# Where the operands of the large products begin in SBUF: a float32 block of delta-net, mixer and merge on one core

## The reference

```python
hdn = rms_norm(x, norm_g) * (1 + scale) + shift           # scale, shift, gate from silu(c) @ ada_w
qkv, z, b, a = split(hdn @ w_in)                          # 1024 x 6176: the delta-net's inputs
...                                                       # conv, silu, l2norm, chunked delta rule, 16 heads
x = x + gate * ((rms_norm(o) * silu(z)) @ w_out)          # 2048 -> 1024
x = rms_norm(x, final_g)
h = rms_norm(x, norm_pre)
proj = h @ w_in_2                                         # differential attention (4 heads) and mLSTM (4 heads)
...
merged = sigmoid(ga) * (ya @ w_a) + sigmoid(gb) * (yb @ w_b)
out = x + rms_norm(merged @ w_out_2, norm_post)
```

## Time and profile before

| | us |
|---|---|
| median of 3 runs | 2098.05 (2096.22 to 2102.33) |
| profiled execution | 2098.08 |
| its span, first to last instruction | 2096.3 |
| PE busy | 1992.0 |
| VectorE busy | 1273.6 |
| ScalarE busy | 853.6 |
| mean granted clock of TensorE | 0.985 |

### The profile page before, as it was taken

The page is one execution under the profiler, slowest core; times in us unless marked ns, Lnnn a source line. Parts: engine busy times, 40 slices in busy tenths (PEclk is TensorE's granted clock), DMA queues, the critical chain, the costliest instruction groups (busy, mean ns, idle before and its releaser), DMA issues.

```text
span 2096.3 us, 29439 instructions
## 1 busy us (share of the span) xinstructions
PE 1992.0 (95%) x11256; PEld 1618.5 (77%) x11256; DVE 1273.6 (61%) x2417; ACT 853.6 (41%) x1377; POOL 138.0 (7%) x114
## 2 busy tenths in 40 slices
PE   5989999999999999969999999999999999999998
PEld 2667878888887888857776787777777678888877
DVE  6777878796869686749625644445353435633543
ACT  4644353544344443149403333535343337600321
POOL 0020202011111212000000000000000000000000
PEclk8999999999999999989999999999999999999999
DMA  7222323232323242548313221120312125211232
GB/s 279 90 76 70 98 78 106 66 101 72 104 68 102 70 121 67 170 148 284 91 43 138 67 66 36 46 95 21 111 41 81 61 79 213 91 50 42 87 114 81
DMA packets 128971, 200.27 MB, mean 96 GB/s; under 512 B 56596, under 2 KB 88084, under 8 KB 127808
## 3 DMA queue, kind: packets, MB, share of 16 engines
q1 hardware_dynamic: 128832, 198.39, 29.6%
HBM read 156.22 MB, written 42.11 MB: 95 GB/s over the span
## 4 chain that ended last, share of the span: by engine, by line
PE 47%; DVE 4%; DMA 2%; issue 2%; ACT 1%; SPq 0%; DVEq 0%; ACTq 0%
PE m_job L1710 6%; PE m_job L1712 6%; PE m_job L1711 6%; PE e_b L2397 4%; PE e_b L2398 4%; PE e_b L2399 4%; PE p_out L1359 2%; PE p_sc L1956 2%; PE p_out L1361 2%; PE p_out L1360 2%; PE p_s L1979 2%; PE e_b L2468 1%; PE e_b L2467 1%; PE e_b L2466 1%; DMA m_raw<-in_w 1%
## 5 line engine op out<-in xcount | busy, mean ns | idle before, releaser
L795 PE MATMUL p_job<-h_hi,w_hi 128*128 128x512 f32 x768 | 321.7, 419 | 18.2 <-DVE h_lo L185 16.8
L797 PE MATMUL p_job<-h_hi,w_lo 128*128 128x512 f32 x768 | 302.6, 394 | 0.0
L796 PE MATMUL p_job<-h_lo,w_hi 128*128 128x512 f32 x768 | 302.1, 393 | 0.0
L1710 PE MATMUL m_job<-h_hi,m_hi 128*128 128x512 f32 x576 | 237.7, 413 | 2.8 <-issue 2.1
L1712 PE MATMUL m_job<-h_hi,m_lo 128*128 128x512 f32 x576 | 227.1, 394 | 0.0
L1711 PE MATMUL m_job<-h_lo,m_hi 128*128 128x512 f32 x576 | 226.0, 392 | 0.0
L795 PEld LDWEIGHTS p_job<-h_hi,w_hi 128*128 128x128 f32 x768 | 146.0, 190 | 59.3 <-issue 16.4
L796 PEld LDWEIGHTS p_job<-h_lo,w_hi 128*128 128x128 f32 x768 | 145.9, 190 | 35.1 <-issue 7.9
L797 PEld LDWEIGHTS p_job<-h_hi,w_lo 128*128 128x128 f32 x768 | 145.6, 190 | 31.3
L1710 PEld LDWEIGHTS m_job<-h_hi,m_hi 128*128 128x128 f32 x576 | 108.8, 189 | 49.8 <-issue 28.3
L633 ACT ACTIVATE pre<-p_job 128x512 f32<-128x512 f32 x96 | 56.7, 591 | 177.6 <-PE p_job L797 174.9
(11 more groups left out here) (398 smaller groups left out, 4170.1 us busy)
## 6 DMA issues: line engine op xcount, KB each, us to landing
w_raw<-in_w SPq DMA_DIRECT2D x49, 512.0 KB, 3.6
m_raw<-in_w SPq DMA_DIRECT2D x49, 512.0 KB, 3.7
rows<-grows SPq DMA_DIRECT2D x32, 512.0 KB, 6.8
ada<-in_ada_w SPq DMA_DIRECT2D x8, 1024.0 KB, 5.3
z_scr<-pre SPq DMA_DIRECT2D x16, 512.0 KB, 2.6
o_scr<-oT SPq DMA_DIRECT2D x64, 128.0 KB, 1.8
ob<-o_scr SPq DMA_DIRECT2D x16, 512.0 KB, 4.9
zb<-z_scr SPq DMA_DIRECT2D x16, 512.0 KB, 4.9
```

Source lines behind the costliest of these rows:

```text
L795: nc.tensor.matmul(bank, hi, h_hi[:, k, cut], start=(k == 0), stop=False)
L796: nc.tensor.matmul(bank, hi, h_lo[:, k, cut], start=False, stop=False)
L797: last = nc.tensor.matmul(bank, lo, h_hi[:, k, cut], start=False, stop=(k == KD - 1))
L1710: nc.tensor.matmul(bank, hi, h_hi[:, k, cut], start=(k == 0), stop=False)
```

## The change

The three small columns `eps`, `gate` and `rin_col` move behind `h_hi`, `h_lo` and the weight tiles, and are declared 64 bytes wide (`LINE` = 16 elements), as is `adt`; their users take slices of the former width. `w_raw`, `w_hi`, `w_lo` are declared for the whole program, and `m_raw`, `m_hi`, `m_lo` become names for the same tiles (they had the same addresses before). The scratch for descriptors shrinks from 16384 to 1024 bytes a partition.

```diff
@@ stage_norm
-            nc.vector.memset(keep["eps"][:], EPS).then_inc(eps_set, 1)
+            nc.vector.memset(keep["eps"][:, 0:1], EPS).then_inc(eps_set, 1)
@@ stage_deltanet
-                                nc.vector.tensor_tensor(keep["gate"][:], gsum[:], gbias[:], ALU.add)
+                                nc.vector.tensor_tensor(keep["gate"][:, 0:KD], gsum[:], gbias[:], ALU.add)
@@ stage_after
-    with ExitStack() as front:
-        for name, shape, dt in (("m_raw", [P, KD * P], F32), ("m_hi", [P, 2, KD * P], F32R),
-                                ("m_lo", [P, 2, KD * P], F32R)):
-            keep[name] = front.enter_context(nc.sbuf_tensor(name, shape, dt))
+    keep["m_raw"], keep["m_hi"], keep["m_lo"] = keep["w_raw"], keep["w_hi"], keep["w_lo"]
@@ build
-            "ident": sb("ident", [P, P]), "ones": sb("ones", [P, P]), "eps": sb("eps", [P, 1]),
-            "gate": sb("gate", [P, KD]), "rin_col": sb("rin_col", [P, NT]),
+            "ident": sb("ident", [P, P]), "ones": sb("ones", [P, P]),
             "h_hi": sb("h_hi", [P, KD, T], F32R), "h_lo": sb("h_lo", [P, KD, T], F32R),
+            "w_raw": sb("w_raw", [P, KD * P]), "w_hi": sb("w_hi", [P, 2, KD * P], F32R),
+            "w_lo": sb("w_lo", [P, 2, KD * P], F32R),
+            "eps": sb("eps", [P, LINE]), "gate": sb("gate", [P, LINE]), "rin_col": sb("rin_col", [P, LINE]),
...
-            for name, shape, dt in (("w_raw", [P, KD * P], F32), ("w_hi", [P, 2, KD * P], F32R),
-                                    ("w_lo", [P, 2, KD * P], F32R), ("tri", [P, P], F32),
-                                    ("conv_w", [P, QK_HEADS, 4, TAPS], F32), ("adt", [P, 3], F32)):
+            for name, shape, dt in (("tri", [P, P], F32), ("conv_w", [P, QK_HEADS, 4, TAPS], F32),
+                                    ("adt", [P, LINE], F32)):
@@ kernel
-    nc = bacc.Bacc("TRN2", target_bir_lowering=False, num_devices=1)
+    nc = bacc.Bacc("TRN2", target_bir_lowering=False, num_devices=1, dynamic_dma_scratch_size=1024)
```

More of the change, by code:

```diff
@@ L35 @@
 EPS = 1e-6
+LINE = 16
 QK_HEADS = 8
@@ L2608, in stage_after @@
     first, second, third = ExitStack(), ExitStack(), ExitStack()
-    with ExitStack() as front:
-        for name, shape, dt in (("m_raw", [P, KD * P], F32), ("m_hi", [P, 2, KD * P], F32R),
-                                ("m_lo", [P, 2, KD * P], F32R)):
-            keep[name] = front.enter_context(nc.sbuf_tensor(name, shape, dt))
[L2613 to L2618, removed]
+    keep["m_raw"], keep["m_hi"], keep["m_lo"] = keep["w_raw"], keep["w_hi"], keep["w_lo"]
+    with first:
+        out = stage_out(nc, io, keep, first)
+    with second:
+        mix = stage_mix(nc, io, keep, second)
+    with third:
+        merge = stage_merge(nc, io, keep, third, mix)
+    if True:
         with nc.Block() as block:
```

## The result

| | before | changed |
|---|---|---|
| median, us | 2097.62 (12 runs, 2095.0 to 2102.33) | 2100.93 (12 runs, 2096.93 to 2107.6) |
| ratio | | 1.0019, 95% interval 1.0011 to 1.0027 |
| profiled execution, us | 2098.08 | 2096.93 |

What follows compares the result with a forecast made beforehand. TensorE's list of 6528 fp32r products was taken as the bound. At 11.3 ns each, delta-net 20, first output product 5.4, mixer 17 and merge 17 sum to 59 us: 2098 - 59 = 2039, rounded to 2040, range 2029 to 2101.

Steps and rivals of the forecast that it cites:

- a loss of 13.3 ns a product: Merge: fp32r products of 512 columns start 226.6 ns apart against 213.3 for the columns; 13.3 ns, 6%, go elsewhere.
- scratch, aliases and small columns cost 0: Whole program: smaller scratch, shared m_* and w_* tiles, and slices of wider small columns were each put at 0 us.
- 17 x 16 = 272: fp32r moving reads: a start at offset 96 of 128 touches 17 lines, costing 272 cycles of 1.2 GHz where 256 are needed.
- I take the 11.3: Each aligned fp32r product in the bound stretches was to gain 11.3 ns, the upper of two bounds; the other was nothing.
- the lines: fp32r products: misaligned starts cost extra memory lines, so alignment makes it faster; forecast 0.34, with rival 1 0.58.
- Rival 2: fp32r products: the 11 ns belong to the weight load or full-rate 4-byte reading, wherever it starts; 2098 us, chance 0.33.
- Rival 3: Some 5000 products: large operands share low address bits at new places, moving reads meet weight reads; 16 us slower, 2114, chance 0.09.
- The 233 of the earlier trace: Mixer, trace before: 7 distances of 233 ns against 226.6 where ScalarE and VectorE are busy; rival 3's evidence.
- Rival 1: Start counts by 128 bytes: moving y at 64 gains nothing, 800 such products in the merge; 2051 us, chance 0.24.
- The share kept in the delta-net: Delta-net, 2222 products: of 25.1 us, 80% kept, 20 us, as a shorter cover for the chunk chain gives some back.
- The mixer's 85%: Mixer, 1776 products: of 20.1 us, 85% kept, 17 us, as PE time partly covers softmax and chunk chains.
- the merge's: Merge, 1568 products: of 17.7 us, 17 kept, with some gaps behind 1980 us.

Runs made afterwards that it cites:

- rel512: The changed kernel with a 320-byte gap behind the small columns, restoring relative offsets of merge and first output product tiles: 2097.14 us, 1.0003 of the kernel before.
- abs32: The kernel before with eps 36 instead of 4 bytes wide, moving everything behind it 32 bytes, relative offsets kept: 2097.3 us against 2096.73, ratio 1.0001.
- apart64: The changed kernel with the 320-byte gap, plus 64 bytes between h_lo and the weights, so some 5300 products stand 64 bytes apart: 2117.45 us, ratio 1.0081.

## Why the prediction was wrong

**Right.** PE bounds nearly all of the time, and a loss of 13.3 ns a product was there: fp32r 226.7, bf16 of the same shape 215.85 in the same array. It belongs to fp32r at the full clock; plain fp32 adds 2 to 3 ns. Whether its removal would be worth 59 us no run shows, since nothing removed it. That scratch, aliases and small columns cost 0 fits rel512, which has them all and takes 1.0003 of the time before.

**The step that failed** is "2048 bytes that begin at offset 96 of a 128-byte line touch 17 lines, and 17 x 16 = 272", and with it "I take the 11.3". 272 is also 256 + 16, which the prediction said, and it called the choice undecided, and then gave the lines 0.58 because they came out without a remainder. The term that failed in the sum is thus 11.3 ns for every product in the bound stretches, 59 us. Measured was 0 for moving `h`, which came to stand on a multiple of 128 (226.7 ns before and after, apart from the settling behind other products), 0 for the whole kernel put on multiples of 128 (abs32, 1.0001), and a loss of 6.6 ns for moving `y` in the merge. One size of product can't tell a sum for each instruction from a share of the bytes, and one offset can't show an effect of offsets. The series show a sum: 32 columns' time at 256, 320, 384 and 512 columns, with both streams on a multiple of 128 as well as elsewhere. Why it is there stays open.

**Rival 2** came true in its main part: the 11 ns stay wherever the product starts. Of its two causes, the weight load is not it in proportion to its columns (at 512 moving columns 32 weight columns are not cheaper). Reading 4-byte data at the full rate fits, since bf16 hasn't the loss and half the clock hides it, but no run isolates it.

**Rival 3** was near in mechanism and named the place wrongly. Its words were that "moving reads meet the weight reads". The runs show that the time depends on how the two lie to each other modulo 256 bytes, 6.7 ns for a product at 64; that the reads meet is its reading of this, and no run looks inside. The 233 of the earlier trace rows on which I had based it are another matter: the offset was 0 there too, and they fit the settling behind plain fp32 products. But `h` and the weights moved together and stayed at offset 0. The large tiles did not all share their low bits after the change: the three columns, padded, now put 192 bytes between the weights and what follows, so `y` came to stand 64 bytes short of a whole 256 to `h`. I had both offsets in the table of the change, 0 and 64 of 128, and read them as absolute ones. 768 products were hit and not 5000: 4.7 us and not 16. (Rival 1's 800 are the moving starts at 64; the 32 sums among them have weights of ones that moved along.)

**Sizes.** The share kept in the delta-net: I counted 80%, apart64 shows 6.2 of 9.8 us, some 60%, in the other direction. The mixer's 85% was 3.2 to 4.9 of 6, with the clock in it, the merge's nearly all as counted.

**The two pages.** abs32 and the changed kernel's moving `h` show no effect of a start at 96 against 0 modulo 128: 226.6 to 227.6 ns. So the trace agrees with the Trainium skill, "SBUF — State Buffer", section "Door 1", as far as the absolute start goes, by whose lines of 16 bytes the change was worth 0; the 6.7 ns of two streams 64 bytes apart are no matter of the absolute start. The other rule, N/2.4 + 2.5 ns in the Trainium skill, "TensorE: Matmul & The Clock Gate", section "Back-to-back issue gap", which gives it for an isolated product, is met by bf16 (215.85 for 215.8) and not by fp32r (226.7).

## What to carry to other kernels

Place the moving tiles and the weight tiles of fp32r products of 512 columns at the same offset modulo 256 bytes; where they begin beyond that made no difference that a run here shows. It is a small thing: 64 bytes between them cost 0.2% of this kernel for 768 products and 0.8% for some 5300. A layout change moves the relative offsets of everything behind it, so compute those before an absolute rule is applied. A gap in the time of one shape should be measured with a second size before it is explained: a sum for each instruction and a share of its bytes look alike at one size. And before a stretch of two traces is compared to a microsecond or two, compare its granted clock: two short drops in the mixer of before looked like a gain of the change.

## What the runs showed that I had not expected

- With 128 weight columns an fp32r instruction takes (N + 32) / 2.4 ns at equal offsets: 226.7, 173.3, 146.6, 119.6 ns for 512, 384, 320, 256 columns, but 202.5 for 448; bf16 215.85 and 109.2 for 512 and 256.
- Weights 4 to 160 bytes behind the moving data modulo 256 cost 4 to 8 ns more at 512 columns, 192 bytes 2.2, 252 bytes 10. At 384 columns 64 bytes cost nothing, at 256 they save 5.5 ns.
- After a plain fp32 product the next fp32r products need two to ten distances to settle at 227, in the series and in the mixer; the mixer's 233 of the earlier trace rows fits that, as the first three distances behind its 105 interruptions average 232 to 233. A busy VectorE alone doesn't do it: in the merge, with VectorE and ScalarE at work, it is 226.6.
- fp32r and bf16 products in turn take 460 ns a pair, 17 more than the two alone.
- fp32r moving data read with a step of two elements takes twice as long, 453 ns.
